# Two places instead of three in the weight ring, ten instead of nine in the ring of gathered rows

## What is computed

```python
for layer in range(DEPTH):                          # DEPTH = 2
    mod_l = jnp.split(jax.nn.silu(c) @ ada_w[layer] + ada_b[layer], 6, axis=-1)      # and mod_c
    p_l = jnp.split(modulate(rmsnorm(x, norm_mix_g[layer]), mod_l[0], mod_l[1]) @ w_in[layer], cuts, axis=-1)
    ...                                             # four head groups: MLA, windowed, neighbourhood, retention
    x = x + mod_l[2][:, None, :] * (y_l @ w_out[layer])
    h2 = modulate(rmsnorm(x, norm_ffn_g[layer]), mod_l[3], mod_l[4])
    x = x + mod_l[5][:, None, :] * peer_ffn(h2, peer_wq[layer], ..., peer_u[layer], peer_v[layer])

def peer_ffn(...):                                  # per token: 8 heads x 16 of 16384 experts
    top_s, pos = lax.top_k(cand_s, 16)
    ...
    a = jnp.einsum("td,tkd->tk", xb, expert_u[eid])
    w = jax.nn.gelu(a, approximate=False) * gate
    return jnp.einsum("tk,tkd->td", w, expert_v[eid])
```

## Time and profile before

| | before |
|---|---|
| median of 3 runs | 4973.56 us (4973.15 to 4980.19) |
| profiled execution, its own time | 4968.76 us |
| its span in the trace | 4967.0 us |
| mean granted PE clock in the span | 0.80 of full speed |
| busy share: PE, DVE, POOL, ACT | 66%, 63%, 30%, 18% |
| moved by DMA | 1496.73 MB, of which 1347.13 MB in the queue of the gathers |
| expert parts, from 905 us to 2945 us and from 3603 us to 4950 us | 3387 us of the span |

### The profile page before, as it was taken

How to read it: one execution, slowest core, us unless ns; L and a number is a source line. 1 busy time by engine, 2 the same in 40 slices (tenths; PEclk the granted TensorE clock), 3 DMA queues, 4 the chain that set the end, 5 groups by cost and what they waited for, 6 DMA issues and landing times.

```text
span 4967.0 us, 49025 instructions
## 1 busy us (share of the span) xinstructions
PE 3289.4 (66%) x16328; PEld 1296.2 (26%) x16328; DVE 3127.8 (63%) x8329; ACT 916.4 (18%) x2477; POOL 1492.6 (30%) x1376
## 2 busy tenths in 40 slices
PE   6989898665786555555555558898877455554554
PEld 1455553331232111111111115555422111111111
DVE  1052332587877878778877861513378787877876
ACT  2152321111111111111111121422111111111211
POOL 0000000233444443444444430000043444444443
PEclk8879889887898777777776768788888877777777
DMA  8100033899999999999999971011299999999998
GB/s 285 36 9 26 22 111 122 336 412 416 406 418 415 401 417 406 412 419 405 418 415 406 415 295 45 1 34 39 75 402 395 414 406 418 404 419 416 400 420 345
DMA packets 290751, 1496.73 MB, mean 301 GB/s; under 512 B 25433, under 2 KB 83929, under 8 KB 126657
## 3 DMA queue, kind: packets, MB, share of 16 engines
q0 software_dynamic: 185888, 1347.13, 65.9%
q1 hardware_dynamic: 73680, 114.85, 6.8%
q10 hardware_dynamic: 30928, 31.61, 1.9%
HBM read 1482.91 MB, written 10.58 MB: 301 GB/s over the span
## 4 chain that ended last, share of the span: by engine, by line
DVE 38%; PE 30%; DMA 19%; issue 7%; ACT 4%; POOL 1%; DVEq 1%; ACTq 0%; POOLq 0%; SPq 0%
DMA X<-in_uv_dram,X 17%; DVE X L1552 16%; PE ps L456 9%; PE ps L823 5%; PE ps L606 2%; DVE X L1563 2%; PE ps L647 2%; PE ps L790 2%; ACT X L1170 2%; PE ps L618 1%; POOL X L1673 1%; DVE X L1471 1%; DVE X L1469 1%; DVE X L1472 1%; DVE X L1559 1%
## 5 line engine op out<-in xcount | busy, mean ns | idle before, releaser
L823 PE MATMUL ps<-X 64*64 64x512 f32 x2560 | 1648.7, 778 | 1399.3 <-DVE X L1563 1384.7
L1673 POOL DMA_INDIRECT X<-in_uv_dram,X x1280 | 1417.2, 1107 | 2194.8 <-PE ps L826 1613.4
L1552 DVE CUSTOM_DVE_ANT_0 X<-yT,X 128x1024 f32<-128x1024 f32 x1280 | 1532.4, 1223 | 338.8 <-DMA X<-in_uv_dram,X 290.0
L826 PE MATMUL ps<-X 64*64 64x512 f32 x2560 | 1649.0, 778 | 0.0
L825 PE MATMUL ps<-X 64*64 64x512 f32 x2560 | 1649.0, 778 | 0.0
L824 PE MATMUL ps<-X 64*64 64x512 f32 x2560 | 1648.8, 778 | 0.0
L823 PEld LDWEIGHTS ps<-X 64*64 64x64 f32 x2560 | 360.5, 163 | 2621.0 <-DVE X L1563 1951.9
L1170 ACT ACTIVATE X<-X 128x1 f32<-128x1 f32 x1280 | 258.6, 203 | 2335.7 <-DVE X L1552 2268.9
L825 PEld LDWEIGHTS ps<-X 64*64 64x64 f32 x2560 | 360.7, 163 | 0.0
L826 PEld LDWEIGHTS ps<-X 64*64 64x64 f32 x2560 | 360.6, 163 | 0.0
L824 PEld LDWEIGHTS ps<-X 64*64 64x64 f32 x2560 | 360.5, 163 | 0.0
(11 more groups left out here) (232 smaller groups left out, 3481.5 us busy)
## 6 DMA issues: line engine op xcount, KB each, us to landing
wring<-in_ada_w_dram SPq DMA_DIRECT2D x48, 1024.0 KB
wring<-in_w_in_dram SPq DMA_DIRECT2D x24, 1024.0 KB
wring<-in_peer_wq_dram SPq DMA_DIRECT2D x24, 1024.0 KB
X<-in_uv_dram,X POOLq DMA_INDIRECT x1280
wring<-in_w_out_dram SPq DMA_DIRECT2D x8, 1024.0 KB
X<-scores ACTq DMA_DIRECT2D x64, 128.0 KB
X<-mods ACTq DMA_DIRECT2D x15, 512.0 KB, 6.7
yT<-mods ACTq DMA_DIRECT2D x8, 512.0 KB
```

The source lines that it names most:

```text
L823: pe.matmul(ps[0:HD, h, :], dg(slice(0, HD), s), v0[0:HD], **ends)
L826: m = pe.matmul(ps[0:HD, 2 + h, :], dg(slice(HD, P), s + 1), v1[HD:P], **ends)
L1552: v.tensor_tensor_reduce(uvr[:, slot, 0:D], h2[:, t, :], uvr[:, slot, 0:D], 1.0, 0.0, ALU.mult, ALU.add, adot[:, s_:s_ + 1]).then_inc(S("d ...
L1673: g.indirect_dma_start(uvr[:, slot, :], None, a["uv"], bass.IndirectOffsetOnAxis(ap=istages[i % 2][:, s:s + 1], axis=0)).then_inc(S(f"uv{s ...
```

## The change

The weight ring gets two places instead of three, and the 8 KB per partition that this frees go to the ring of gathered rows, which gets ten instead of nine. `X` grows by 8 KB, and the places of the expert part that lay behind `uvr` move up by 8 KB. No instruction is added or removed; the waits move.

```diff
-WRING = 3
+WRING = 2
...
-UVRING = 9
+UVRING = 10
...
-        X_WORDS = 101 * 256
+        X_WORDS = 109 * 256
...
-        qTb = view(72 * K, [2, NLAT]); stage = view(76 * K, [2, NLAT])
+        qTb = view(80 * K, [2, NLAT]); stage = view(84 * K, [2, NLAT])
...
-        small = view(87 * K, [D]); gjunk = view(91 * K, [D])
+        small = view(95 * K, [D]); gjunk = view(99 * K, [D])
...
-        dgs = view(99 * K, [DGRING, HD]); gtab = view(95 * K, [4, NCTX]); final_gain = hT[:, 0:4, 0:NCTX]
+        dgs = view(107 * K, [DGRING, HD]); gtab = view(103 * K, [4, NCTX]); final_gain = hT[:, 0:4, 0:NCTX]
```

More of the change, by code:

```diff
@@ L312, in build @@
         uvr = view(0, [UVRING, 2 * D])
-        qTb = view(72 * K, [2, NLAT]); stage = view(76 * K, [2, NLAT])
[L314 to L318, removed]
+        qTb = view(80 * K, [2, NLAT]); stage = view(84 * K, [2, NLAT])
+        scn = view(88 * K, [2, 2, NKEYS])
+        tk = view(90 * K, [2, NKEYS]); cand = view(91 * K, [TOPK, TOPK]); cand2 = view(92 * K, [TOPK * TOPK])
+        oh = view(93 * K, [TOPK, TOPK]); v12 = view(94 * K, [2, TOPK]); i12 = view(94 * K + 32, [2, TOPK], U32)
+        i12f = view(94 * K + 64, [2, TOPK]); pos = view(94 * K + 96, [TOPK], U32); pab = view(94 * K + 112, [2, TOPK], U32)
+        pabf = view(94 * K + 144, [2, TOPK]); sel = view(94 * K + 176, [2, TOPK]); gs = view(94 * K + 208, [2, PH])
         mod_early = (view(36 * K, [2, CH]), view(96 * K, [2, CH]))
```

## The result

The changed kernel takes 5019.1 us (median of 4 runs, 5009.0 to 5023.8), the kernel before 4973.4 us beside it: ratio 1.0088, 95% interval 1.0075 to 1.0101. It is 46 us slower, where 4981 us was forecast with a range up to 4997 us. The profiled execution took 5017.7 us (span 5015.9 us, against 4967.0 us before). Of the 48.9 us between the spans, the first gathered row of layer 0 lands 54.0 us later (974.2 for 920.2 us), and the ten tiles of the expert parts, added up, are 5.3 us shorter (3355.5 for 3360.8 us, from landing to landing).

What follows compares the result with a forecast made beforehand. Gather DMA was taken to bound the expert parts, PE work the rest, with load waits in the modulation. Profiled 4968.8 us + 22 lost - 15 gained = 4975.8 us; on the median 4980.6 us, range 4964 to 4997 us.

Steps and rivals of the forecast that it cites:

- the loss of the weight place: Modulation: with two weight places PE waits longer for loads, 22 us lost in all, bounds 16 to 26.
- the walk: Modulation, chunk by chunk: a lone load usable after about 5.2 us, a queued one 2.7 us later; sum 22 us.
- The forecast's four stretches: Modulation: start 8 us, layer 1's chunks 0 to 4 6 us, chunks 5 and 6 3 us, layer 1's 7 to 11 5 us.
- A change of the granted clock in the stages between: Stages between the modulation stretches: named as a sign of a wrong forecast, not contained in the sum; no size given.
- The durations of the loads: Weight loads: 5.2 us alone, 2.7 us behind another in a queue, about ten times as long during the gathers.
- The estimate of 4.4 us: Modulation: a 1 MB load alone by 2.0 us plus bytes at 436 GB/s; the walk then gives 15 us.
- The tenth place: Expert parts: one more gather queued when the consumer stalls, 15 us gained, bounds 0 to 25.
- The 2.5 us for layer 1's first tile: Layer 1's first tile, where DMA dips to 250 GB/s: the tenth place gains a full gather, 2.5 us.
- The 1.5 us for each change: Eight tile changes, five in layer 0 and three in layer 1: the tenth place gains 1.5 us at each.
- The second rival: Expert parts: the slowest DMA engine sets landings, so the ring pays nothing; 22 us loss alone, 4996 us; chance 0.14.
- The first rival: Expert tiles: choosing experts every 16 gathers drains the queue, so the tenth place gains 35 to 40 us, 4958 us; chance 0.17.
- Query weights: Gathers: PE's waits for `peer_wq` put at 0, at most 4 us; rival of late loads 4997 us, chance 0.05.

Runs made afterwards that it cites:

- busy waits: The changed kernel with 40 extra TensorE products placed in PE's waits for modulation weight loads, no load moved: 5004.0 us, ratio 1.0054.
- short fills: The changed kernel with 16 extra products, in smaller groups meant to fit inside PE's waits for modulation weights: 5000.8 us, ratio 1.0052.
- the lent first layer: The changed kernel plus a third weight place, lent from the expert part's region for the first 24 weight loads only: 5001.5 us, ratio 1.0053.
- six quarters: The changed kernel with four 4 KB weight places plus two lent for the first 128 quarter loads: 4958.1 us; with nine ring places 4961.6 us.

## Why the prediction was wrong

**The failed step is the loss of the weight place, 22 us (bounds 16 to 26), measured at 46 to 54 us.** Its mechanism, where it happens, and the waits themselves were right: PE's waits for `in_ada_w` grew by 25.3 us. The forecast's four stretches of 8, 6, 3 and 5 us grew by 18.4, 11.7, 4.3 and 12.0 us. What the sum lacked was a term for PE's own work, which it put at nothing: the walk used 1.0 us for a half and 3.0 us for the group of L474, L476 and L510, which the earlier trace rows show at the full clock, although show the same half at 1.9 us. Behind the longer waits of these runs the lower level is granted more often, and the same products took 24 us more. The busy waits and the short fills show that the clock costs time and that filled waits keep it up: with the waits filled it is 1.00 in the first layer's chunks 8 to 11, and 12 to 18 us come back while PE has more to do. In the profiles 7 to 8 us of that (busy waits) and 14 to 15 us (short fills) lie in the stretches with extra products; the rest can be variation between executions. That all 24 us of longer products hang on the two places was not shown, and three places had such a phase too (the lent first layer, 5.7 us). The 7.6 us of the first profile's 54.0 that lie between the stretches have no cause that was shown. "A change of the granted clock in the stages between" was named as what could make it wrong; the change came in the modulation itself.

**A slip of the sum.** The walk has chunks 0 and 1 of layer 1 3.4 us late and, behind L716, 3.1 + 2.6 + 0.6 = 6.3 us for chunks 2 to 4; the sum takes 6 us for the two together. Measured, it is 7.5 us more up to L716 and 4.2 us more behind it.

**The durations of the loads held.** A load alone took 5.0 to 5.5 us in the changed kernel, the second of two issued together 7.0 us. The estimate of 4.4 us by the formula of the Trainium skill (DMA: Bandwidth & Descriptors, Anatomy of one DMA), which is for GpSimd's path, is less than any load here took. During the gathers a load took 26 to 27 us, which is five times a load alone and not ten, as the forecast says; ten it is against the 2.7 us between two loads in a queue.

**The tenth place, 15 us forecast, is worth 5 to 8 us in two of three profiles.** In eight profiles the ten tiles add up to 3353.4 to 3355.5 us with ten places, in three to 3360.8, 3361.0 and 3365.9 us with nine; the third makes it 10 to 13 us. The medians of whole runs differ by 3.4 to 6.9 us with two weight places and by 3.5 us with six quarters. The 2.5 us for layer 1's first tile were right (2.3 us). The 1.5 us for each change were not: that was a choice between 0 and 2.4, and at the change shown the last part lost only 0.5 us; layer 0's five changes together gave back 0.4 us, layer 1's three 2.6 us. The second rival had this mechanism. Its forecast that the dips go away was wrong; they stay, and they are in the other parts.

**The first rival's mechanism is real, one place further down.** Nine places are just enough for the choice of experts every 16 gathers; eight lose 84 us. The 8.5 us of a tile that the rival hoped for did not come: a tile of layer 0 takes 329.1 and 328.9 us.

**Query weights.** PE waited once, 0.4 us, for `in_peer_wq` (L790). The estimate of 0 was right.

**The stages between** kept their lengths up to 7.6 us in all, 3 of which vary between executions as well.

## What to carry to other kernels

A buffer taken from a short product loop cost twice here: the wait, and the products after it at the lower granted clock. A walk that prices waits with durations from a stretch at the full clock gives the first half only; take the durations at both levels as bounds. Cut the buffer finer before you take it away, and look for memory that another phase leaves free: the same 16 KB in four places lost 6 us where two places lost 46 us, and with 8 KB lent it beat both kernels. The ring of gathers was worth 84 us up to the longest regular pause of its consumer and 5 to 13 us of 3360 beyond it, and that had to be read at the last part of each gather, not at the mean of the DMA engines.

## What was not expected of the hardware

The sixteenth part of a gather landed 4.5 us behind the fifteenth at the change shown (gather 135 of the changed kernel, 1339.46 against 1335.00 us), with the next gathers like it, and its pace of 2.49 us was the pace of the dot products. The deeper the ring, the further the last part lags: over the gathers with all 16 parts in the trace it lands 0.4 us behind the fifteenth in the median with eight places, 0.8 to 1.0 us in the three profiles with nine and 2.3 to 2.9 us in the eight with ten. That suggests that the places gained hold mostly gathers of which one part is missing; it was not tested. The lower granted clock cost one period of chunks 5.3 us for 3.0 us of products, and 16 extra products, 10.0 us in all, placed in waits, gave back 15 to 18 us. Between two executions of the changed kernel the first gather moved by 4 us, and by 8 us to that of the two places with a ring of nine, with the slow phases in different places.
